# First layer's two convolved projections run side by side, with the gate rows ahead of the convolution

## What is computed

```
mod = silu(c) @ w_ada + b_ada; sh1, sc1, g1, sh2, sc2, g2 = split(mod, 6)
h = rms_norm(x, norm1_g) * (1 + sc1) + sh1
q_a, k_a, v_a, qk_m, v_m, o_m, gates = split(h @ w_in)
attn = head_norm(attention(rope(q_a), rope(k_a), v_a))
qk_m = silu(causal_conv(qk_m, conv_w, conv_b)); q_m, k_m = split(qk_m)
hm = head_norm(mlstm(q_m, k_m, v_m, gates)) * sigmoid(o_m)
x = x + g1 * (concat(attn, hm) @ w_out)
x = x + g2 * experts(rms_norm(x, norm2_g) * (1 + sc2) + sh2)
```

## Time and profile before

| | |
|---|---|
| median of 3 runs | 1299.67 us (1299.21 to 1300.42) |
| the profiled execution, its own time | 1298.47 us |
| its span, first to last instruction | 1296.6 us |
| mean granted TensorE clock | 0.958 |
| busy: PE, DVE, ACT | 1114.9, 669.8, 549.5 us |
| chain that ended last | PE 56%, DMA 22%, DVE 13%, ACT 7% |

### The profile page before, as it was taken

The page is one execution under the profiler, slowest core; times in us unless marked ns, Lnnn a source line. Parts: engine busy times, 40 slices in busy tenths (PEclk is TensorE's granted clock), DMA queues, the critical chain, the costliest instruction groups (busy, mean ns, idle before and its releaser), DMA issues.

```text
span 1296.6 us, 20056 instructions
## 1 busy us (share of the span) xinstructions
PE 1114.9 (86%) x8501; PEld 842.7 (65%) x8501; DVE 669.8 (52%) x1422; ACT 549.5 (42%) x1202; POOL 0.2 (0%) x4
## 2 busy tenths in 40 slices
PE   6999999876666675756789999999999979999997
PEld 4777668544333542524456677888887758888886
DVE  4565765211110111111167756998876867777765
ACT  4554553211011110111155665666654755666653
POOL 0000000000000000000000000000000000000000
PEclk9999999999797897889899999999999999999999
DMA  9996848999999999999997457677757515554510
GB/s 391 420 427 273 363 192 349 412 428 427 427 426 427 423 428 427 427 427 426 426 421 283 160 217 278 241 275 291 294 220 295 231 66 202 200 189 189 195 33 33
DMA packets 29847, 397.36 MB, mean 306 GB/s; under 512 B 3512, under 2 KB 4920, under 8 KB 5432
## 3 DMA queue, kind: packets, MB, share of 16 engines
q1 hardware_dynamic: 29320, 395.72, 74.7%
q10 hardware_dynamic: 432, 0.30, 0.1%
HBM read 394.97 MB, written 1.05 MB: 305 GB/s over the span
## 4 chain that ended last, share of the span: by engine, by line
PE 56%; DMA 22%; DVE 13%; ACT 7%; issue 2%; ACTq 0%; DVEq 0%; SPq 0%
PE ps L1217 17%; DMA ring<-in_w13b 12%; PE ps L1221 9%; DMA mem<-in_w 7%; PE ps L1211 5%; PE ps L1213 4%; PE ps L1212 4%; DVE memr L2533 4%; ACT mem L2006 4%; PE ps L1796 3%; DVE mem L2533 3%; ACT memr L2006 3%; PE ps L1732 3%; PE ps L1251 3%; DMA mem<-in_w13b 2%; DVE mem L2539 2%
## 5 line engine op out<-in xcount | busy, mean ns | idle before, releaser
L2533 DVE TENSOR_TENSOR memr<-ring,memr 128x512 fp32r<-128x512 f32 x432 | 292.0, 689 | 158.3 <-ACT memr L2006 154.8
L2006 ACT ACTIVATE memr<-ring 128x512 fp32r<-128x512 f32 x432 | 265.2, 629 | 187.9 <-PE ps L1213 78.7
L1217 PE MATMUL ps<-memr 128*128 128x512 f32 x1056 | 275.3, 394 | 3.3 <-DVE memr L2533 2.0
L2006 ACT ACTIVATE mem<-ps 128x256 f32<-128x256 f32 (+5 forms) x294 | 121.6, 433 | 340.0 <-PE ps L1796 219.7
L1217 PEld LDWEIGHTS ps<-memr 128*128 128x128 f32 x1056 | 186.7, 189 | 36.5 <-DVE memr L2539 5.0
L1211 PE MATMUL ps<-memr 128*128 128x256 f32 (+2 forms) x504 | 175.4, 348 | 4.8 <-DVE memr L2533 3.4
L1213 PE MATMUL ps<-memr 128*128 128x256 f32 (+2 forms) x504 | 165.1, 328 | 0.0
L1212 PE MATMUL ps<-memr 128*128 128x256 f32 (+2 forms) x504 | 165.0, 327 | 0.0
L2533 DVE TENSOR_TENSOR mem<-mem,ps 128x512 f32<-128x512 f32 (+1 forms) x76 | 43.5, 572 | 233.6 <-ACT mem L2006 233.6
L1221 PEld LDWEIGHTS ps<-memr 128*128 128x128 f32 x1056 | 151.4, 190 | 16.5 <-DVE memr L2539 0.9
L1221 PE MATMUL ps<-memr 128*128 128x256 f32 x1056 | 156.9, 282 | 0.9 <-DVE memr L2539 0.5
(11 more groups left out here) (190 smaller groups left out, 1007.5 us busy)
## 6 DMA issues: line engine op xcount, KB each, us to landing
ring<-in_wpk SPq DMA_DIRECT2D x89, 2048.0 KB, 8.5
ring<-in_w13a SPq DMA_DIRECT2D x17, 2048.0 KB, 44.9
mem<-in_w13b SPq DMA_DIRECT2D x16, 2048.0 KB, 46.2
ring<-in_w SPq DMA_DIRECT2D x16, 2048.0 KB, 45.6
ring<-in_w13b SPq DMA_DIRECT2D x15, 2048.0 KB, 43.3
mem<-in_w SPq DMA_DIRECT2D x15, 2048.0 KB, 45.2
mem<-in_w13a SPq DMA_DIRECT2D x15, 2048.0 KB, 44.6
mem<-in_wpk SPq DMA_DIRECT2D x1, 2048.0 KB, 10.4
```

Of the source, the lines that this page charges most:

```text
L1217: return self.e.matmul(ps[:, 0:512], a[0], b[1], start=start, stop=stop)
L2006: return self.e.activation(out, src, f, **k)
L2533: return self.e.tensor_tensor(out, a, b, op)
```

## The change

It has five parts. The loads of w_in unit 4 and unit 6 come ahead of ada (0,4) and (0,5). tile_in packs the two convolved units anew: the first of them in the list holds the slabs of kk = 0 to 3 of both projections in turn, the second those of kk = 4 to 7. modulate_x issues two splits behind chunk 1 and two behind chunk 2, and in the second half two behind chunk 5 and two behind chunk 6; between the halves hold keeps any split back. first_half issues eight slabs (kk = 0 to 3 of conv0 and conv1 in turn) with the products of (0,1) and (0,3) behind the fourth; the rest of the slabs follow the chunks in the same way. conv_copy(0), gate_weights, conv_copy(1) and gates then stand behind all sixteen slabs, (0,4) behind the gates, and the jobs are gate_rows, conv(0), conv(1), in that order and all from there on.

```diff
--- before.py
+++ after.py
@@ -407,7 +407,7 @@
             packed(u, n)
 
     ada = lambda i, n: (U_ADA + 12 * i + n, 0)
-    mixed(ada(0, 0), ada(0, 2), (U_IN + 3, 8), ada(0, 1), ada(0, 3), ada(0, 4), (U_IN + 4, 8), ada(0, 5), (U_IN + 6, 8),
+    mixed(ada(0, 0), ada(0, 2), (U_IN + 3, 8), ada(0, 1), ada(0, 3), (U_IN + 4, 8), (U_IN + 6, 8), ada(0, 4), ada(0, 5),
           ada(0, 6), ada(0, 7), (U_IN + 5, 8), ada(0, 8), ada(0, 9), (U_IN, 8), ada(0, 10), (U_IN + 1, 8), ada(0, 11),
           ada(1, 0), (U_IN + 2, 8), ada(1, 1), ada(1, 2), (U_OUT, 8), ada(1, 3), (U_OUT + 1, 8))
     for e in range(32):
@@ -708,11 +708,14 @@
             if held is not None:
                 self.h_low(tag, held)
             held = c
-            if split and 0 < c < 4:
-                self.stage(1)
+            if split and 0 < c < 3:
+                self.stage(2)
             if c == 1 and not split:
                 self.hold = False
                 self.stage()
+            if split and c in (5, 6):
+                self.hold = False
+                self.stage(2)
         if held is not None:
             self.h_low(tag, held)
 
@@ -1026,32 +1029,35 @@
     p.late_loads()
 
     low = lambda tag: lambda k: (s.dve_h, ("low", tag, k))
-    conv_step = p.project_T_steps("conv0", m.h2, low((0, 0)), 256, 128)
+    conv_steps = [p.project_T_steps(f"conv{u}", m.h2, low((0, 0)), 256, 128) for u in range(2)]
 
     def first_half():
         p.warm(4, low((0, 0))(0))
-        for _ in range(4):
-            next(conv_step)
-        p.ada_mm(0, 1)
-        p.ada_mm(0, 3)
-        p.ada_copy()
-        p.ada_close(True)
-        p.ada_mm(0, 4)
+        for k in range(4):
+            for step in conv_steps:
+                next(step)
+            if k == 1:
+                p.hold = True
+                p.ada_mm(0, 1)
+                p.ada_mm(0, 3)
+                p.ada_copy()
+            if k == 2:
+                p.ada_close(True)
 
     p.pad_conv()
-    p.modulate_x(0, 0, "n0", {4: first_half, 7: p.ada_copy})
-    for _ in conv_step:
-        pass
+    p.modulate_x(0, 0, "n0", {4: first_half})
+    for k in range(4):
+        for step in conv_steps:
+            next(step)
+    p.last = p.spent - 1
     p.conv_copy(0)
     p.gate_weights()
-    p.jobs.append(p.conv(0))
-    p.side.append(p.work())
-    p.project_T("conv1", m.h2, low((0, 0)), 256, 128)
     p.conv_copy(1)
     p.gates()
-    p.jobs += [p.conv(1), p.gate_rows()]
-    if not p.side:
-        p.side.append(p.work())
+    p.jobs += [p.gate_rows(), p.conv(0), p.conv(1)]
+    p.side.append(p.work())
+    p.ada_mm(0, 4)
+    p.ada_copy()
     p.ada_unit(0, 5)
     p.step_side()
     p.project_T("om", m.h2, low((0, 0)), 256, 128)
@@ -3417,6 +3423,13 @@
     return np.stack([tile_rows(w[:, c:c + 512]) for c in range(0, w.shape[1], 512)])
 
 
+def tile_in(w):
+
+    t = tile_cols(w[:, 0:3584])
+    t[3:5] = t[3:5].reshape(2, 128, 8, 512).transpose(2, 0, 1, 3).reshape(2, 8, 128, 512).transpose(0, 2, 1, 3).reshape(2, 128, 4096)
+    return t
+
+
 def tile_pairs(w):
     h = w.shape[1] // 2
     return np.stack([tile_rows(np.concatenate([w[:, c:c + 256], w[:, h + c:h + c + 256]], 1)) for c in range(0, h, 256)])
@@ -3466,7 +3479,7 @@
         "wgt": tile_rows(i["w_in"][0][:, 3584:3592]),
         "wpk": np.concatenate(
             [tile_ada(i["w_ada"][0], 0), tile_ada(i["ada_w_2"][0], 1), tile_ada(i["ada_w_2"][1], 2),
-             tile_cols(i["w_in"][0][:, 0:3584]), tile_list(i["w_out"][0], [(4, 8), (0, 4)]),
+             tile_in(i["w_in"][0]), tile_list(i["w_out"][0], [(4, 8), (0, 4)]),
              tile_pairs(i["a_w_qkv_2"][0][:, 0:2048]), tile_cols(i["a_w_qkv_2"][0][:, 2048:3072]),
              tile_list(i["a_w_o_2"][0], [(0, 4), (4, 8)]), tile_cols(i["b_w_qkv_2"][0]),
              tile_list(i["b_w_o_2"][0], [(0, 4), (4, 8)])]
```

## The result

| | before | after |
|---|---|---|
| median, 15 runs each | 1300.09 us (1298.82 to 1301.61) | 1303.17 us (1301.01 to 1306.76) |
| ratio, 95% interval | | 1.0024 (1.0017 to 1.0030) |
| profiled execution, own time; span | 1298.47; 1296.6 | 1302.72; 1300.9 |
| mean granted clock | 0.958 | 0.953 |

The kernel became slower by 3.1 us, just over the 0.2% (2.6 us) that a measurement can tell. The forecast of 1302.1 was for 2.4 us over the before shown then, which was 0.4 us lower than the one here. In after, the lines of the code stand 6 higher: L1211 is L1217, L1251 is L1257, L1278 is L1284, L2006 is L2012, L2011 is L2017, L2533 is L2539, L2539 is L2545, L1438 is L1444, L1446 is L1452. In runs whose edit adds lines they stand one or two higher again.

What follows compares the result with a forecast made beforehand. TensorE paces the first layer, with q0's landing fixed by DMA; experts last as long as their bytes. Halves −0.6 and −2.2, gates +2.6, kmt +2.7 less 0.0 to 0.3 give +2.4 us: 1302.1, range 1299.0 to 1303.9.

Steps and rivals of the forecast that it cites:

- main case: Whole kernel: likeliest 1302.1 us, own range 1301.2 to 1303.0, chance 0.60.
- same: Whole kernel: outcome within 0.2%, or 2.6 us, of before; chance 0.50.
- slower: Whole kernel: outcome slower by more than 0.2%, or 2.6 us; chance 0.42.
- Halves: Projection slabs before the gates: first half gains 0.6 us, second half 2.2, together 2.8.
- Gates: Gate product: gate_w's makers stand behind slab 15, so PE stands still 2.6 us and gates start at 55.07.
- om at 61.6: Start of om's product behind the gates, (0,4) and (0,5): 61.6 against 61.8, leaving 0.2 us of the gain.
- kmt: Transposes of kmt: wait for the last SiLU behind q0's first split, start 97.7 instead of 95.2, +2.5 us.
- rival 1: Before kmt: taps stand earlier in the queues, so kmt doesn't wait and the time is 1299.5; chance 0.13.
- PE would be there at 95.0 and stands still 2.7 us: TensorE before kmt: done with its earlier work at 95.0, then idle 2.7 us until the SiLU ends at 97.7.
- The landing: q0's unit: may land up to 0.3 us earlier because om's slot is released 1.5 us sooner; +2.4 taken.
- Rival 3: TensorE at kmt: a pause halves the clock for two windows, about 1.7 us, time 1303.8; chance 0.10.
- Table load: ACT's LOG_EXP load of 1.28 us moves to 97.7, before q0's fifth split; hidden with 0.9 us to spare.

Runs made afterwards that it cites:

- e2: Changed kernel with gate_weights issued between the second and third pair of the second half's slabs: 1303.89 us, ratio 1.0037 to before.
- e8: e4 with vm's unit loaded ahead of conditioning unit (0,7) and q0's ahead of (0,9): 1297.90 us, ratio 0.9980 to before.
- e13: The changed kernel, unedited, measured and profiled a third time: 1304.28 us, ratio 1.0029 to before.
- e12: The changed kernel, unedited, measured and profiled once more: 1304.07 us, ratio 1.0030 to before.
- e6: Changed kernel with gate_rows and the two convolutions as two side lists stepping together: 1301.86 us, ratio 1.0011 to before.
- e1: Changed kernel with the jobs in the order conv(0), conv(1), gate_rows: 1305.33 us, ratio 1.0040 to before.
- e4: Changed kernel with the edits of e2 and e6 together: 1300.37 us, ratio 1.0002 to before.
- e10: Changed kernel with 18 calls of throwaway products on the identity ahead of kmt's wait: 1305.62 us, ratio 1.0040 to before.
- e14: Changed kernel with throwaway products before gates (9 calls) and kmt's wait (10), and one group doubled in each of the last two experts: 1303.27 us, ratio 1.0021.
- e3: Changed kernel with q0's unit loaded one place earlier, ahead of ada (0,9): 1302.79 us, ratio 1.0027 to before.
- e9: As e8, but gates and the start of gate_rows behind the second half's third slab pair, convolution jobs behind ada (0,5): 1297.55 us, ratio 0.9980 to before.
- e11: Changed kernel with 5 calls of throwaway products on the identity ahead of kmt's wait: 1303.49 us, ratio 1.0030 to before.

## Why the prediction was right, and where it was not

The direction, the size within 0.7 us (3.1 against 2.4) and both new waits were right, and the time lay in the range. It lay 0.2 us above the main case's own range (to 1303.0), and "same" had been given 0.50 against 0.42 for "slower", which came.

*Halves.* Right within 0.1 us (the forecast's figure in brackets): slabs from 24.74 (24.82), turn 36.11 (36.1), chunk operations 37.49 (37.5), last slab 52.5 (52.4). The forecast's terms give 2.9 us rather than 2.8 (57.15 less 54.25), a matter of rounding. That the gain is real is shown by e2, where om starts 3.0 us early, and by e8, which keeps 2.4 of them.

*Gates.* Right: 55.02 (55.07), by the chain as it was written down: split, remainder, zeroing, ACT's copies, DVE. TensorE stood still 2.5 us (2.6).

*om at 61.6.* It was 63.1 in the profiled execution, and 61.4 in e13, the same kernel, where the clock held. The difference is the clock.

*kmt.* The step counting was right. Behind q0's first split stand four remainders and fourteen taps in DVE's timeline, as counted. The forecast had 11.7 us from that split to kmt. From the landing, at most 0.03 us ahead of the split, it was 11.73 in after and 11.74 in e2, e12 and e13. e6 keeps every operation, moves only where they stand, and removes the wait: the order of the queues binds, as argued against rival 1, not DVE's load. "PE would be there at 95.0 and stands still 2.7 us" is what e13 shows (95.07, 2.65). One sign was off: ACT waited 1.8 us for q0's unit in after and not about 4, which changes nothing, as the chain starts at the landing.

*The landing,* the term that was mis-sized: "up to 0.3 us earlier", for which the sum went from +2.5 to +2.4. It was 86.58 in after and 85.7 to 86.4 in nine other executions whose load order and start are the same up to there (e1, e2, e4, e6, e10 to e14), 86.02 in before. So no shift towards earlier shows, as the freed om slot should have brought; it is scatter of some 0.4 us about the beat, and it passes whole to kmt. With after's own landing, 0.56 us later than before's, the +2.5 is +3.1, which is kmt's distance in that profile. With e14's, 0.06 later, it is 2.6, and 2.7 was measured.

*The clock,* the other part. Rival 3 had 0.10, priced 1.7 us, at kmt, as a thing that happens or does not. It happens in part of the executions, at either pause. At the gates it costs nothing more, as kmt hangs on the landing: after and e12 have the fall there and stand 3.2 and 2.9 us behind before. At kmt it costs 5.7 − 2.5 = 3.2 us (e13: the shift behind the slow stretch less that of kmt itself, 97.72 against 95.2), and 3.2 again in e3 (5.2 − 2.0), about half of the 6.8 us (98.6 to 105.4 in e13) that ran at 0.50. I had priced it by two windows of 2 us, of which half would have been 2.0 and not 1.7. What I held against the rival, the 2.65 us of pauses at 173 to 190, was in several pieces; here 2.1 to 2.7 us in one piece were enough. The Trainium skill, "TensorE: Matmul & The Clock Gate", section "Why this matters for your kernels", warns of idle gaps between bursts of matmuls. The traces bear it out in e13 (2.65 us of pause) and e3 (2.1), but not in e2 and e4, where the clock held behind 3.2 and 2.8 us. If the 8 of 28 executions over 1305 us are those with the fall, at +3.2 each, the mean rises by 0.9 us, and the median by less. That is an estimate; it would do for the rest, 3.1 against 2.7.

*Table load.* Right as priced: after's load took 1.28 us at 98.28, the next ACT operation began at 99.57, and nothing waited. e9 adds that with the waits gone fewer loads gain nothing.

*What I left out* is not of the change but of its mending: e4 shows that a gain ahead of a DMA on a fixed beat stops at the next unit. To see it, the landing of vm's unit (71.1) had to be laid beside the time at which TensorE would want it.

## What to carry to other kernels

When engines take instructions strictly in order, a prefetch that waits for a DMA holds up everything issued behind it; list what stands behind it at each step, and count from the landing. Time won upstream of such a landing is kept only if the transfer is moved forward too (here two units by one place in the load order: e4 without it is level with before, e8 with it 2.6 us faster). Independent chains of short side work belong beside each other, not behind each other, if two consumers at the same place need both (e6: 0.8 us behind before in place of 3.2). And a pause of TensorE like the ones here, 2.1 to 3.9 us, should be priced with its clock, as a chance of a longer loss, not as its length alone.

## What was not expected of the hardware

- The clock fell to half behind one unbroken pause of 2.1 us (e3), 2.7 us (e13) or 3.9 us (e1), but not always: after the same pause of 2.5 us at the gates it fell in after, e10, e11 and e12 and held at 1.00 in e1, e3, e6 and e13. Even 3.2 us (e2, at kmt) and 2.8 us (e4, in vm) left it at 1.00 in the executions profiled.
- It went with the moment at which TensorE had begun: in the four with the fall at the gates the first conditioning product began at 12.6 to 13.2 us, in the four without at 13.5 to 14.0; the three falls at kmt or the transposes ahead of it (e1, e3, e13) are all of the second kind. So the moment of a pause seems to matter beside its length. No run varied that start on purpose; this stays open.
- The stretch at half clock can outlast the pause that brought it: 6.8 us in e13 behind a pause of 2.7, so that the fall cost 3.2 us, more again than the pause. It isn't always so long: 3.4 us in e1 (98.2 to 101.6).
